# Running sums of the state-space pairs spread over 256 columns instead of 384, the causal mask applied to C*B, and the own row's sum subtracted on GpSimd

## What is computed

```
def ssd_scan(xdt, la, bm, cm):          # 32 heads in 4 groups, chunks of 128
    def step(state, inp):
        acs = jnp.cumsum(lac, axis=1)
        seg = acs[:, :, None] - acs[:, None, :]
        lmat = jnp.where(mask, jnp.exp(jnp.where(mask, seg, 0.0)), 0.0)
        cb = jnp.einsum('bign,bjgn->bijg', cc, bc)
        y = jnp.einsum('bijgr,bjgrp->bigrp', cb[..., None] * lmat, xc)
        ...
```

## Time and profile before

| | us |
|---|---|
| median of 3 runs | 2184.87 (2182.55 to 2184.94) |
| the profiled execution | 2182.6 |
| its span | 2180.8 |
| TensorE busy | 2148.3 |
| VectorE busy | 1641.6 |
| ScalarE busy | 1206.1 |
| GpSimd busy | 0.5 |

### The profile page before, as it was taken

The page is one execution under the profiler, slowest core; times in us unless marked ns, Lnnn a source line. Parts: engine busy times, 40 slices in busy tenths (PEclk is TensorE's granted clock), DMA queues, the critical chain, the costliest instruction groups (busy, mean ns, idle before and its releaser), DMA issues.

```text
span 2180.8 us, 48183 instructions
## 1 busy us (share of the span) xinstructions
PE 2148.3 (99%) x18868; PEld 2086.8 (96%) x18868; DVE 1641.6 (75%) x2651; ACT 1206.1 (55%) x1829; POOL 0.5 (0%) x5
## 2 busy tenths in 40 slices
PE   9999999999999999999999999999999999999998
PEld 8999999998999999899999999999899999999998
DVE  7987777997768776778956877776678956877764
ACT  6646544555555445446647855445446647855444
POOL 0000000000000000000000000000000000000000
PEclk9999999999999999999999999999999999999999
DMA  7434555644346556554554456556554553455553
GB/s 247 155 127 137 197 191 185 199 159 150 130 151 213 191 190 208 175 168 151 166 176 134 136 194 205 188 187 212 176 168 146 173 175 126 139 193 186 187 185 134
DMA packets 102976, 376.55 MB, mean 173 GB/s; under 512 B 11680, under 2 KB 11808, under 8 KB 102304
## 3 DMA queue, kind: packets, MB, share of 16 engines
q1 hardware_dynamic: 101664, 368.66, 51.9%
q10 hardware_dynamic: 1152, 5.58, 0.7%
HBM read 373.14 MB, written 1.05 MB: 172 GB/s over the span
## 4 chain that ended last, share of the span: by engine, by line
PE 86%; DVE 8%; ACT 3%; issue 2%; DMA 1%; SPq 0%; DVEq 0%; ACTq 0%
PE acc L699 24%; PE acc L700 24%; PE acc L701 24%; DVE w_lo L1733 3%; PE acc L818 1%; PE acc L820 1%; PE acc L819 1%; ACT w_hi L1255 1%; PE mid L1157 1%; PE mid L1055 1%; PE mid L1140 1%; DMA w_raw<-weights_d 1%; DVE pr L2480 1%; DVE branch L2217 0%; DVE s_lo L2488 0%
## 5 line engine op out<-in xcount | busy, mean ns | idle before, releaser
L1733 DVE TENSOR_TENSOR w_lo<-w_raw,w_hi 128x1024 fp32r<-128x1024 f32 x694 | 845.8, 1223 | 297.6 <-ACT w_hi L1255 291.2
L1255 ACT CAST w_hi<-w_raw 128x1024 fp32r<-128x1024 f32 x694 | 724.9, 1047 | 523.2 <-PE acc L701 477.4
L699 PE MATMUL acc<-h_hi,w_hi 128*128 128x256 f32 x2080 | 597.0, 287 | 0.0
L700 PE MATMUL acc<-h_lo,w_hi 128*128 128x256 f32 x2080 | 585.5, 282 | 0.0
L701 PE MATMUL acc<-h_hi,w_lo 128*128 128x256 f32 x2080 | 582.4, 280 | 0.0
L699 PE MATMUL acc<-g_hi,w_hi 128*128 128x256 f32 x1472 | 416.6, 283 | 0.0
L700 PE MATMUL acc<-g_lo,w_hi 128*128 128x256 f32 x1472 | 412.2, 280 | 0.0
L701 PE MATMUL acc<-g_hi,w_lo 128*128 128x256 f32 x1472 | 411.9, 280 | 0.0
L699 PEld LDWEIGHTS acc<-h_hi,w_hi 128*128 128x128 f32 x2080 | 391.8, 188 | 7.5 <-issue 6.2
L700 PEld LDWEIGHTS acc<-h_lo,w_hi 128*128 128x128 f32 x2080 | 393.4, 189 | 0.5
L701 PEld LDWEIGHTS acc<-h_hi,w_lo 128*128 128x128 f32 x2080 | 393.8, 189 | 0.0
(11 more groups left out here) (452 smaller groups left out, 3391.7 us busy)
## 6 DMA issues: line engine op xcount, KB each, us to landing
w_raw<-weights_d SPq DMA_DIRECT2D x695, 512.0 KB, 3.4
p<-p_d ACTq DMA_DIRECT2D x3, 1080.0 KB, 9.3
rdec<-decay_d ACTq DMA_DIRECT2D x2, 768.0 KB, 5.1
p<-p_d SPq DMA_DIRECT2D x1, 1024.0 KB, 11.1
out_d<-work SPq DMA_DIRECT2D x4, 256.0 KB, 2.4
x_all<-x_d SPq DMA_DIRECT2D x1, 516.0 KB, 4.4
w_raw<-weights_d SPq DMA_DIRECT2D x2, 256.0 KB, 6.0
x_all<-x_d SPq DMA_DIRECT2D x1, 512.0 KB, 6.5
```

The costliest lines, as they stand in the source:

```text
L699: mm(dst, wh, hi[:, k, :], start=first and j == 0, stop=False)
L700: mm(dst, wh, lo[:, k, :], start=False, stop=False)
L1255: nc.scalar.copy(w_hi[:, slot, :], w_raw[:, slot, :]).then_inc(hi_done, 1)
L1733: tt(w_lo[:, slot, :], w_raw[:, slot, :], w_hi[:, slot, :].bitcast(F32), SUB).then_inc(lo_v, 1)
```

## The change

The running sums are spread over the columns once: `sums` now has 256 columns, and both heads of a pair share one bank, `mid[b % 2]`, in 2 x 256 columns. The second half of a head's 384 columns is the same running sum as columns 128 to 255 with another row's own sum taken off, so it is no longer made by TensorE. The bf16 matmuls are gone. ScalarE copies the 512 columns to `lseg` in SBUF ("sums" task), which now has two buffers. GpSimd writes the second half of each head from columns 128 to 255, then the first half in place, each as (value minus own sum, then minimum with 0): four `tensor_scalar` instructions a pair, with a wait on its own first two in between. ScalarE then runs one Exp over 768 elements in place. The minimum keeps the masked part at or below 1, and the mask is a factor in C*B: VectorE's copy of C*B (L2452) becomes a product with the 0/1 matrix `tri`. The "sums" task of pair b stands one slab earlier, behind slab `RO_S + 3 * (b // 2) + b % 2 - 1`.

```diff
@@ tasks2
         i = RO_S + 3 * (b // 2) + b % 2
-        after.setdefault(i, []).extend([("sums", b)] if b % 2 == 0 else [])
-        after.setdefault(i + 1, []).extend([("sums", b + 1)] if b % 2 == 0 else [])
+        after.setdefault(i - 1, []).append(("sums", b))
         after.setdefault(i, []).append(("pair", b))
@@ buffers
-        lseg = in_arena("lseg", 41984, [P, 2, TRI])
+        lseg = in_arena("lseg", 38912, [P, 2, 2, TRI])
-        sums = in_arena("sums", 97280, [P, TRI], F32R)
+        sums = in_arena("sums", 97280, [P, T], F32R)
@@ gpsimd, for both layers and b = 0 to 15
+            def differences(at, b):
+                pool.wait_ge(a_bc, at.n * 16 + (b + 1))
+                if b == 0:
+                    pool.wait_ge(v_dt, at.n * 4 + 4)
+                late, all_ = lseg[:, b % 2, :, T:TRI], lseg[:, b % 2, :, 0:T]
+                for n in range(2):
+                    last = nc.gpsimd.tensor_scalar(late[:, n, :], all_[:, n, P:T], dts[:, 9, 1, 2 * b + n:2 * b + n + 1], 0.0,
+                                                   ALU.subtract, ALU.min)
+                last.then_inc(p_late, 1)
+                pool.wait_ge(p_late, at.n * 16 + (b + 1))
+                for n in range(2):
+                    last = nc.gpsimd.tensor_scalar(all_[:, n, :], all_[:, n, :], dts[:, 9, 0, 2 * b + n:2 * b + n + 1], 0.0,
+                                                   ALU.subtract, ALU.min)
+                last.then_inc(p_seg, 1)
@@ tensor, sums_of_pair
-                if b:
-                    pe.wait_ge(a_l, at.n * 16 + b)
-                else:
+                if b >= 2:
+                    pe.wait_ge(a_bc, at.n * 16 + (b - 1))
+                elif b == 0:
...
                 for n in range(2):
                     pick = sel[:, 2 * b + n:2 * b + n + 1].to_broadcast([P, P])
-                    mm(mid[n][:, 0:TRI], pick, sums[:, :], start=True, stop=False)
-                for n in range(2):
-                    for lo in (0, T):
-                        last = mm(mid[n][:, lo:lo + P], unit[:, :], above[:, :], start=False, stop=lo == T)
+                    last = mm(mid[b % 2][:, n * T:(n + 1) * T], pick, sums[:, :], start=True, stop=True)
@@ scalar
+            def pair_sums(at, b):
+                act.wait_ge(pe_bc, at.n * 16 + (b + 1))
+                if b >= 2:
+                    act.wait_ge(v_m, at.n * 16 + (b - 1))
+                elif b == 0:
+                    act.wait_ge(v_dt, at.n * 4 + 4)
+                nc.scalar.copy(lseg[:, b % 2, :, 0:T], mid[b % 2][:, :].rearrange("p (n t) -> p n t", n=2)).then_inc(a_bc, 1)
             def pair(at, b):
-                act.wait_ge(pe_bc, at.n * 16 + (b + 1))
...
-                for n in range(2):
-                    h = 2 * b + n
-                    nc.scalar.activation(lseg[:, n, 0:T], mid[n][:, 0:T], ACT.Exp, bias=dts[:, 9, 0, h:h + 1])
-                    last = nc.scalar.activation(lseg[:, n, T:TRI], mid[n][:, T:TRI], ACT.Exp, bias=dts[:, 9, 1, h:h + 1])
-                last.then_inc(a_l, 1)
+                act.wait_ge(p_seg, at.n * 16 + (b + 1))
+                nc.scalar.activation(lseg[:, b % 2, :, :], lseg[:, b % 2, :, :], ACT.Exp).then_inc(a_l, 1)
@@ vector, c_times_b
-                copy(cbm[:, g, :], mid[0][:, 0:TRI]).then_inc(v_cb, 1)
+                tt(cbm[:, g, :], mid[0][:, 0:TRI], con2("tri"), MUL).then_inc(v_cb, 1)
```

More of the change, by code:

```diff
@@ L391, in hybrid_kernel @@
         sq2 = in_arena("sq2", 61440, [P, 4, T])
-        sqz = in_arena("sqz", 35840, [P, 4, T])
+        sqz = in_arena("sqz", 33792, [P, 4, T])
         s_hi = in_arena("s_hi", 61440, [P, NI, T], F32R)
@@ L411, in hybrid_kernel @@
         cbm = place("cbm", [P, SG, TRI], at=p_at + 4 * P2_N)
-        above_at = c1_at + 4 * (C1["rope_c"][0] + C2_N)
-        above = place("above", [P, P], BF16, at=above_at)
-        unit = place("unit", [P, P], BF16, at=above_at + 2 * P)
-        assert P2_N + SG * TRI <= P1_N and C2_N + P <= C1_N - C1["rope_c"][0]
+        assert P2_N + SG * TRI <= P1_N and C2_N <= C1_N - C1["rope_c"][0]
         def par1(name, a=0, b=None):
@@ L469, in hybrid_kernel @@
         params = sem("params")
-        v_above = sem("v_above")
+        v_sel = sem("v_sel")
         pad_ok = sem("pad_ok")
@@ L550, in hybrid_kernel @@
         pe_bc = sem("pe_bc")
+        a_bc = sem("a_bc")
+        p_late = sem("p_late")
+        p_seg = sem("p_seg")
         a_l = sem("a_l")
@@ L650, in _ @@
             nc.gpsimd.memset(zpad[:, :], 0.0).then_inc(pad_ok, 1)
+            def differences(at, b):
[12 more added lines that the diff above has]
+                last.then_inc(p_seg, 1)
+            for n in range(DEPTH):
+                at = Layer(True, n)
+                for b in range(NI):
+                    differences(at, b)
         @block.tensor
@@ L1120, in c_times_b @@
                     pe.wait_ge(consts2, 16)
-                    pe.wait_ge(v_above, 1)
                     pe.wait_ge(a_xs, at.n * XB + XB)
@@ L1592, in dt_sums @@
                 act.wait_ge(a_xs, at.n * XB + XB)
-                nc.scalar.copy(sums[0:2 * SH, 0:T], mid[0][0:2 * SH, P:P + T])
-                nc.scalar.copy(sums[0:2 * SH, T:TRI], mid[0][0:2 * SH, T:P + T]).then_inc(a_dt, 1)
-            def pair(at, b):
-                act.wait_ge(pe_bc, at.n * 16 + (b + 1))
-                if b:
-                    act.wait_ge(v_m, at.n * 16 + b)
-                else:
-                    act.wait_ge(v_dt, at.n * 4 + 4)
-                for n in range(2):
-                    h = 2 * b + n
-                    nc.scalar.activation(lseg[:, n, 0:T], mid[n][:, 0:T], ACT.Exp, bias=dts[:, 9, 0, h:h + 1])
-                    last = nc.scalar.activation(lseg[:, n, T:TRI], mid[n][:, T:TRI], ACT.Exp, bias=dts[:, 9, 1, h:h + 1])
-                last.then_inc(a_l, 1)
+                nc.scalar.copy(sums[0:2 * SH, :], mid[0][0:2 * SH, P:P + T]).then_inc(a_dt, 1)
+            def pair_sums(at, b):
[5 more added lines that the diff above has]
+                nc.scalar.copy(lseg[:, b % 2, :, 0:T], mid[b % 2][:, :].rearrange("p (n t) -> p n t", n=2)).then_inc(a_bc, 1)
+            def pair(at, b):
+                act.wait_ge(p_seg, at.n * 16 + (b + 1))
+                nc.scalar.activation(lseg[:, b % 2, :, :], lseg[:, b % 2, :, :], ACT.Exp).then_inc(a_l, 1)
             def z_square(at, b):
@@ L1696, in _ @@
                         dt_sums(at)
+                    elif task[0] == "sums":
+                        pair_sums(at, task[1])
                     elif task[0] == "pair":
@@ L2322, in _ @@
             dve.wait_ge(consts2, 16)
-            copy(unit[:, :], con1("ident"))
             nc.vector.memset(sel[2 * SH:P, :].bitcast(F32), 0.0)
-            tt(sel[0:2 * SH, :], con1("ident")[0:2 * SH, 0:SH], con1("ident")[0:2 * SH, SH:2 * SH], ADD)
-            ts(above[:, :], con2("tri")[:, 0:P], -1.0, 1e30, ADD, MUL).then_inc(v_above, 1)
+            tt(sel[0:2 * SH, :], con1("ident")[0:2 * SH, 0:SH], con1("ident")[0:2 * SH, SH:2 * SH],
+               ADD).then_inc(v_sel, 1)
             def turned(at, own, i):
@@ L2394, in dt_sums @@
                 nc.vector.memset(sums[2 * SH:P, :].bitcast(F32), 0.0)
-                ts(dts[:, 9, :, :], mid[0][:, 2 * SH:4 * SH].rearrange("p (r h) -> p r h", r=2), -1.0, None, MUL)
+                copy(dts[:, 9, :, :], mid[0][:, 2 * SH:4 * SH].rearrange("p (r h) -> p r h", r=2))
                 lo = sums[SH:2 * SH, :]
-                tt(lo[:, 0:T], mid[0][SH:2 * SH, P:P + T], lo[:, 0:T].bitcast(F32), SUB)
-                tt(lo[:, T:TRI], mid[0][SH:2 * SH, T:P + T], lo[:, T:TRI].bitcast(F32), SUB).then_inc(v_dt, 1)
+                tt(lo, mid[0][SH:2 * SH, P:P + T], lo.bitcast(F32), SUB).then_inc(v_dt, 1)
             def ret_scores(at, h):
@@ L2460, in pair @@
                     dve.wait_ge(v_cb, at.n * 4 + 4)
-                tt(mt[:, :, :], lseg[:, :, :], cbm[:, b // 4, :].unsqueeze(1).to_broadcast([P, 2, TRI]), MUL).then_inc(v_m, 1)
+                both = cbm[:, b // 4, :].unsqueeze(1).to_broadcast([P, 2, TRI])
+                tt(mt[:, :, :], lseg[:, b % 2, :, :], both, MUL).then_inc(v_m, 1)
             def pair_y(at, b):
```

1 line of the change is left out of this document (added).

## The result

The kernel before took 2182.90 us (median of 6 runs, 2180.79 to 2184.94), the changed kernel **2228.73 us** (6 runs, 2227.29 to 2230.63): ratio 1.0213, with a 95% interval of 1.0202 to 1.0223. It is 46 us slower. The profiled execution took 2227.29 us, with a span of 2225.5.

The account below looks back on a forecast made before the run. The prediction took TensorE to bound the kernel: 11.4 us saved there, less 2.0 us for ScalarE's waits for GpSimd in dense periods, gave -9.4 us, from 2184.87 to 2175.5 us; range 2171 to 2184.

Parts of the forecast that it names:

- the TensorE saving: On TensorE, each of 32 pairs loses four bf16 mask matmuls and 128 sum columns: 0.36 us a pair, 11.4 us in all.
- the order: Odd pair's sums one slab group earlier, so its Exp runs in ScalarE's former idle time: about 0.7 us back.
- GpSimd's own time: A pair's four GpSimd instructions between ScalarE's copy and Exp, without interference: 1.5 us taken, between 1.04 and 2.1.
- The interference: Extra time of a pair's four GpSimd instructions from waiting behind VectorE's instructions: 1.1 us.
- The wide end of the prediction: Upper bound on a pair's GpSimd time: 2.1 us, plus each instruction queued behind a 1.22 us VectorE instruction, 7.0 us.
- G: GpSimd's time for one pair, between ScalarE's copy and its Exp: taken as 2.6 us.
- For the even pair ... over 4 us: hidden: On ScalarE, the even pair's copy comes a slab and a table load before its Exp, so GpSimd's time costs nothing.
- A layer then loses 5 x (G - 3.4) + 3 x (G - 1.45) - 3: Loss in us per layer once G exceeds 3.4: five quiet periods, three dense (group norm) ones, less 3 us slack.
- the odd wait: ScalarE's wait for GpSimd before odd Exps: G - 1.3 = 1.3 us, against idle time of 2.1 (quiet), 0.15 (dense periods).
- GpSimd bounding ScalarE: Rival: from G = 4.0 us ScalarE's waits for GpSimd outweigh the gain; at 4.5 us +11.9 us, 2196.8; chance 0.11.
- Exclusion: Rival: VectorE's products and weight remainders stand while GpSimd holds the shared SBUF access: -5.4 us, 2179.5; chance 0.15.
- The sums did get shorter: Answers the rival that a fixed cost keeps TensorE's two sum matmuls at 0.35 us: -7.7 us; no chance given.

## Why the prediction was wrong, point by point

*Forecast 2175.5 us, range 2171 to 2184, slower with a chance of 0.11: it came out at 2228.7.* The direction was wrong, and the measured time lies 45 us above the range.

**What bounds the kernel, and the TensorE saving: right.** 11.4 us forecast, 11.7 measured with nothing on GpSimd. Its parts are less clean: 6.4 for the mask, where 7.7 stood, and part of it is only collected because the order moves. The prediction gave the order 0.7 us; by the medians it is 3 to 4.

**The term of GpSimd's own time: the first failure.** "1.5 us of its own, between 1.04 and 2.1". It is 3.7 us, above the upper bound. That bound was a memset's price, doubled for reading, two operations and a scalar. No row of before showed a GpSimd instruction that reads or computes, and a doubled price of a write was no bound for it: per element the instruction costs four times the memset's (3.4 ns against (0.32 - 0.10)/263 = 0.84 ns from the earlier trace rows). The interference, 1.1 us, was nearly right: 5.2 - 3.7 = 1.5 us with the hand-overs. The wide end of the prediction, 7.0 us, did enclose G = 5.2, but by waits alone, and the range of times did not follow it: at 4.5 us the text had 2196.8 and gave it 0.11.

**"For the even pair ... over 4 us: hidden": failed too.** The row at 1153.89 and the Exp, free to start at 1158.41, leave 3.86 us from GpSimd's start at 1154.55. G is larger, so ScalarE waits 1.34 us there. Cover was counted from the copy's start, without the copy and the hand-over, and against the taken G, not against its upper bound.

**"A layer then loses 5 x (G - 3.4) + 3 x (G - 1.45) - 3": too small even with the right G.** Put in both layers against the saving it gives about -11 us at 2.5, -4 at 3.5 and +23 at 5.2; measured were -6, +7 and +46. It charged the odd wait only, and took 3 us of slack a layer from idle time that had its place elsewhere. In the changed kernel's quiet period the waits are 1.34 + 4.03 = 5.37 us, the idle time there was 2.1 us, and the difference, 3.3 us, is what the period grew by over the forecast 11.04 us (14.46 - 11.04 = 3.42). So in quiet periods the idle time was a good account once both waits are in it. In the three dense periods the two waits are 4.6, 4.9 and 4.9 us against the 0.15 us of idle time; by the same account a period is 15.7 us, and the even pairs' products (1205.76 to 1252.48) give 15.57. So the account holds there too. The traces do not show the forecast's 3 us of slack a layer, and it is the dense part that lost most.

**The rivals.** The mechanism that happened is the last, GpSimd bounding ScalarE. It was dismissed since "it needs both a doubled instruction time and a wait of 0.6 us ahead of each one"; the own time was 2.5 times the taken one. Exclusion did not happen. The sums did get shorter.

**What was named as a sign** holds: the odd wait was to be over 2.1 us for the forecast to be wrong, and is 4.03; TensorE's waits for products were to pass 4 us in the two stretches, and are 23.9 us in the first layer's stage. The two sums take 0.34 us behind the values, less than the 0.42 forecast.

## What to carry to other kernels

A step moved to an idle engine is a link in a chain before it is relief: write the loop down (copy, other engine, consumer, next copy), add up its links over a period, and compare that with the period of the engine that bounds. If no row shows the new instruction on that engine, its price has no upper end from a memset; let the range reach to where the loop closes, or measure the instruction in a probe first. And the same work can gain 9 us or lose 4 by its place alone: give it to the engine that is not between two halves of the same pair.

## What the runs showed of the hardware

GpSimd's tensor-scalar with two operations, its scalar in memory, costs 0.28 us for one element and 3.4 ns for each further one of a row; a copy of 256 takes 0.40 us and a memset 0.31. VectorE does it from PSUM in 0.48 us. A reading GpSimd instruction gets longer by up to 1.3 us beside VectorE, which itself gets longer by some 0.2 us at most. Behind a stall of 2.45 us TensorE's granted clock was 0.50.
